# A block of two layers on one core: one weight ring of eight, a fourth pair by seven products, and low parts made by an adding DMA

## The chip, the cores and the metric

The kernel runs on one core of a Trainium2 chip. The core has five engines with queues of their own: TensorE (PE) multiplies matrices into PSUM, VectorE (DVE) and ScalarE (ACT) work elementwise, GpSimd (POOL) does some copies and issues DMAs, SyncE (SP) only issues DMAs. They meet at semaphores. 16 DMA engines move data. The metric is the device time of one execution in microseconds.

## What is computed

256 tokens of 2048 channels go through one transformer-like block and one mixer block, all in float32:

```python
h = rms_norm(x, norm_mix)
proj = h @ w_in                                   # 2048 x 11264
y_a = hgrn2_mixer(...); y_b = chunked_relpos_attention(...)
merged = gate_a * (y_a @ w_proj_a) + gate_b * (y_b @ w_proj_b)
x = x + merged @ w_out
h = rms_norm(x, norm_ffn)
ff_gate, ff_up = split(h @ w_ffn_in)              # 2048 x 11264
x = x + (silu(ff_gate) * ff_up) @ w_ffn_out       # 5632 x 2048
h = rmsnorm(x, a_norm_2)
u, v, gate = split(h @ a_w_in_2)                  # 2048 x 12288
v = rmsnorm(gelu(v), a_v_gain_2)
y = gelu(u) * (a_w_s_2 @ v + a_b_s_2)             # by groups of 512 channels
x = rmsnorm(x + (y * silu(gate)) @ a_w_out_2, final_norm_2)
```

## The kernel before

**Three matmuls for one.** Each float32 operand is written as a high part, rounded to the type fp32r, and a low part, the rest. A product is then high x high + low x high + high x low (`three` in the code): three matmuls. The activations' two parts stay in SBUF (`a_hi`, `a_lo`). The weights stream. A **unit** is a slab of 256 rows x 512 columns of weights (512 KB): a load into `raw`, then `split` on ScalarE copies it to `w_hi` (L615), `split` on VectorE subtracts to get `w_lo` (L1194), then TensorE uses it in 12 matmuls of 512 columns. `raw`, `w_hi` and `w_lo` are rings of `RING = 4` units. The high part of unit j+4 is made when unit j is used (`unit_used`), the load of unit j waits for the low part of unit j-4 (`lo_ready`, L485).

**Segments and steps.** All matrix work is a list of segments `S` (L347), each cut into steps of two column blocks. In form "D" the units of the two blocks alternate and two neighbouring units make a **pair**: feed-forward input (`FFN_IN`, 11 steps of 8 pairs), feed-forward output (`FFN_OUT`, 2 steps of 22), v (`V_IN`, 4 steps of 8), u and gate (`UG_IN`, 8 steps of 8), half of the last product (`Y_FIRST`), and a part of the input projection (`AV`).

**Seven products.** A pair is a 2x2 by 2x2 block product: 8 block products, 24 matmuls. Some pairs are done by seven (Strassen's scheme in Winograd's form), 21 matmuls, `mixed_pair`. The price lies on the other engines: four sums of weight blocks on VectorE (`weight_sums`, L1413 to L1416, from `raw` to `t_sum`, one of them in place in `raw`), their high part on ScalarE (`t_hi`, L746) and their low part on VectorE (`t_lo`, L1426), all in buffers for one pair. Sums of activation blocks (`s_sum`, `s_hi`, `s_lo`) are made once a stage. At the end of a step, `parts` (L1435 to L1438) and `whole` (L1450, two additions for each half) put the banks `mx` and `gp` together. Which pairs are done so is a table: `MIXED = (2, 4, 6)`, in step 0 of feed-forward input (4, 6), in step 0 of v (6,).

**The order** is written out by hand. Each engine has its own loop over units j = 0 to 15 of a step, calling `double_ahead` (work for unit j+4) and a `mid` function for what else falls there. The turn of the feed-forward output of step i-1 (eight transposes, `turn_ff`, L2226, into banks of `mx`, copied out by `ff_copy` on ScalarE) stands at unit 1 of step i. On GpSimd, the load of `ws_raw` (L589) waits until all activation parts of feed-forward input are made (`op_ready`), which the last `s_lo` (L1684) of row block 3 completes in step 0, and the load of `bs_all` comes next.

## Time and profile before

| | us |
|---|---|
| runs: median (lowest to highest of 3) | 2148.54 (2147.5 to 2149.36) |
| span of the profiled execution | 2146.8 |
| TensorE busy | 2135.6 (10176 matmuls) |
| VectorE busy | 1742.5 |
| ScalarE busy | 1261.2 |
| GpSimd busy | 138.1 |
| DMA | 412.35 MB, mean 192 GB/s |

The span goes from the first to the last instruction of one execution. Busy time counts an engine's own instructions; matmuls overlap in a pipeline, so a busy TensorE says little by itself, and the distance between the starts of two matmuls says what one costs. Shares over the whole span mix stages; the views of one step below say more.

### The profile page before, as it was taken

The page shows a single profiled execution, that of the slowest core. Times are in us where ns is not written, and L with a number is a line of the kernel's source. Part 1 is how long each engine was busy: PE and PEld are TensorE (multiplying, and loading weights), DVE is VectorE, ACT ScalarE, POOL GpSimd, SP SyncE. Part 2 cuts the span into 40 slices and gives each one's busy share as a digit, 9 for nine tenths or more (in the row PEclk, how much of TensorE's full clock was granted, in tenths as well). Part 3 has the DMA queues.
Part 4 walks back from the last instruction along what each step waited for, and adds up shares of the span by engine and source line. Part 5 has one row for each costly group of instructions (what it writes and reads, how often), then busy time and mean ns, then how long its engine had stood idle before and what let it go on. Part 6 is the DMA issues. An engine that isn't in the chain of part 4 may idle for free.

```text
span 2146.8 us, 30208 instructions
## 1 busy us (share of the span) xinstructions
PE 2135.6 (99%) x10176; PEld 1788.8 (83%) x10176; DVE 1742.5 (81%) x2125; ACT 1261.2 (59%) x1483; POOL 138.1 (6%) x218
## 2 busy tenths in 40 slices
PE   9999999999999999999999999999999999999998
PEld 9988888888888888888888888888888888888886
DVE  6578788666565698999899887787889999999886
ACT  6465455465544665555555555557667666666565
POOL 2022433101000000000000000000000000000000
PEclk9999999999999999999999999999999999999999
DMA  7666555575555566666666666666666666656664
GB/s 254 182 189 211 157 157 150 174 236 174 183 186 181 186 205 199 198 196 198 203 188 196 200 193 199 192 204 187 206 206 187 188 193 194 193 180 208 203 193 152
DMA packets 211513, 412.35 MB, mean 192 GB/s; under 512 B 13176, under 2 KB 13280, under 8 KB 211296
## 3 DMA queue, kind: packets, MB, share of 16 engines
q1 hardware_dynamic: 208608, 402.70, 60.9%
q0 software_dynamic: 1920, 5.31, 0.8%
q10 hardware_dynamic: 896, 3.15, 0.5%
q8 instruction: 55, 0.90, 0.2%
q14 instruction: 34, 0.28, 0.0%
HBM read 409.01 MB, written 3.16 MB: 192 GB/s over the span
## 4 chain that ended last, share of the span: by engine, by line
PE 96%; DVE 2%; DMA 1%; ACT 0%; issue 0%; DVEq 0%; SPq 0%; ACTq 0%
PE gp L1983 49%; PE gp L1915 33%; PE mx L1983 10%; PE mx L2226 1%; PE mx L2110 1%; DVE w_lo L1194 1%; DMA raw<-a_w_out_in 1%; PE mx L2275 1%; DVE t_lo L1426 0%; DVE ff_lo L1193 0%; PE mx L2113 0%; DMA x_tok<-x_in 0%; PE mx L2107 0%; PE mx L2162 0%; PE mx L2206 0%
## 5 line engine op out<-in xcount | busy, mean ns | idle before, releaser
L615 ACT ACTIVATE w_hi<-raw 128x1024 fp32r<-128x1024 f32 x759 | 797.1, 1056 | 681.6 <-PE gp L1915 246.3
L1194 DVE TENSOR_TENSOR w_lo<-raw,w_hi 128x1024 fp32r<-128x1024 f32 x759 | 921.2, 1230 | 233.8 <-ACT w_hi L615 224.1
L1983 PE MATMUL gp<-w_hi,a_hi 128*128 128x512 f32 x1053 | 413.3, 393 | 0.0
L1983 PE MATMUL gp<-w_lo,a_hi 128*128 128x512 f32 x1053 | 410.1, 389 | 0.0
L1983 PE MATMUL gp<-w_hi,a_lo 128*128 128x512 f32 x1053 | 409.8, 389 | 0.0
L1983 PEld LDWEIGHTS gp<-w_hi,a_hi 128*128 128x128 f32 x1053 | 197.7, 188 | 43.0 <-issue 2.9
L1983 PEld LDWEIGHTS gp<-w_lo,a_hi 128*128 128x128 f32 x1053 | 197.6, 188 | 41.4
L1983 PEld LDWEIGHTS gp<-w_hi,a_lo 128*128 128x128 f32 x1053 | 197.8, 188 | 39.8
L1915 PE MATMUL gp<-w_hi,a_hi 128*128 128x512 f32 x576 | 229.9, 399 | 0.0
L1915 PE MATMUL gp<-w_lo,a_hi 128*128 128x512 f32 x576 | 224.6, 390 | 0.0
L1915 PE MATMUL gp<-w_hi,a_lo 128*128 128x512 f32 x576 | 224.3, 389 | 0.0
L1983 PE MATMUL gp<-w_hi,ff_hi 128*128 128x512 f32 x410 | 159.9, 390 | 0.0
L1983 PE MATMUL gp<-w_lo,ff_hi 128*128 128x512 f32 x410 | 159.5, 389 | 0.0
L1983 PE MATMUL gp<-w_hi,ff_lo 128*128 128x512 f32 x410 | 159.5, 389 | 0.0
L1426 DVE TENSOR_TENSOR t_lo<-t_sum,t_hi 128x1536 fp32r<-128x1536 f32 x76 | 133.5, 1756 | 8.0 <-ACT t_hi L746 3.8
L1915 PEld LDWEIGHTS gp<-w_lo,a_hi 128*128 128x128 f32 x576 | 108.1, 188 | 23.1
L1915 PEld LDWEIGHTS gp<-w_hi,a_hi 128*128 128x128 f32 x576 | 108.2, 188 | 22.1 <-DVE w_lo L1194 0.4
L1915 PEld LDWEIGHTS gp<-w_hi,a_lo 128*128 128x128 f32 x576 | 108.3, 188 | 21.2
L746 ACT ACTIVATE t_hi<-t_sum 128x1536 fp32r<-128x1536 f32 x76 | 111.9, 1473 | 0.0
L1983 PEld LDWEIGHTS gp<-w_lo,ff_hi 128*128 128x128 f32 x410 | 76.9, 188 | 16.1
L1983 PEld LDWEIGHTS gp<-w_hi,ff_hi 128*128 128x128 f32 x410 | 77.0, 188 | 15.9
L1983 PEld LDWEIGHTS gp<-w_hi,ff_lo 128*128 128x128 f32 x410 | 77.0, 188 | 15.7
(420 smaller groups left out, 3305.3 us busy)
## 6 DMA issues: line engine op xcount, KB each, us to landing
raw<-a_w_in_in SPq DMA_DIRECT2D x192, 512.0 KB, 4.5
raw<-w_ffn_in_in SPq DMA_DIRECT2D x176, 512.0 KB, 4.5
raw<-w_in_in SPq DMA_DIRECT2D x175, 512.0 KB, 3.9
raw<-w_ffn_out_in SPq DMA_DIRECT2D x88, 512.0 KB, 4.6
raw<-a_w_out_in SPq DMA_DIRECT2D x64, 512.0 KB, 4.9
raw<-w_out_in SPq DMA_DIRECT2D x32, 512.0 KB, 4.0
raw<-w_proj_a_in SPq DMA_DIRECT2D x16, 512.0 KB, 4.6
raw<-w_proj_b_in SPq DMA_DIRECT2D x16, 512.0 KB, 4.7
```

The costliest lines, as they stand in the source:

```text
L615: act.activation(w_hi[:, slot], raw[:, slot], ACT.Copy).then_inc(hi_ready, 1)
L746: act.activation(t_of(k)[1][:], t_of(k)[0][:], ACT.Copy).then_inc(t_hi_ready, 1)
L1194: dve.tensor_tensor(w_lo[:, slot], raw[:, slot], w_hi[:, slot], ALU.subtract).then_inc(lo_ready, 1)
L1426: dve.tensor_tensor(t_of(k)[2][:], t_of(k)[0][:], t_of(k)[1][:].bitcast(F32), ALU.subtract).then_inc(t_lo_ready, 1)
L1915: ins = pe.matmul(out_, stat, mov, start=start, stop=last and p == 2, skip_group_check=True)
L1983: ins = pe.matmul(out_, stat[sp_], mov[mp], start=start and p == 0, stop=stop and p == 2, skip_group_check=True)
L2110: pe.matmul(part8[:, (l + 1) * P:(l + 2) * P], decay[buf][:, l, tb], decay[buf][:, l, tb], start=True, stop=True, skip_group_check=True)
L2226: ins = pe.transpose(turn_b[:, m, t * P:(t + 1) * P], src(t, m), ident[:])
L2275: ins = pe.matmul(mx[:, c // 2, t0:t0 + P], v_one[:, b, c * P:(c + 1) * P], ws_t[:, b, bass.ds(g, 1)].rearrange("p a n -> p (a n)"), start ...
```

## The change

1. **One ring of eight.** `raw` and `w_lo` become one ring of eight slots, `w_lo` written over `raw`; `w_hi` keeps four. A load of unit j waits until unit j-8 is used.
2. **The sums moved up.** `weight_sums` of a pair stands ahead of the low part before it, one `split` earlier.
3. **Pair 0 by seven products** (`MIXED_WIDE`) in every step but the first of feed-forward input and v. Its sums are made at the end of the step before. The additions `whole(1)` move from unit 15 to unit 13 of the order, ahead of `t_lo`. Row block 0 gets sums of activations too (`SUMS0`, `s0_hi`, `s0_lo`). The turn moves from unit 1 to unit 15 of step i.
4. **Four low parts a step by DMA** (`ADDED`: units 3, 7, 11, 15 of feed-forward input, from unit 7 of step 0 on). ScalarE writes minus the high part to `low` (two buffers), GpSimd issues a DMA that adds `raw` to it, TensorE does the unit's 8 matmuls with high weights first and its 4 with `low` last (`low_last`). On VectorE a `memset` of one column stands in its place, to keep the count of `lo_ready`.
5. The scratch for GpSimd's DMAs is set to 8192 bytes, the last step of v stands outside the loop on VectorE and ScalarE.

```diff
+MIXED_WIDE = (0, 2, 4, 6)
+ADDED = (3, 7, 11, 15)
+LOWS = 2
...
-        raw = new("raw", [RING, UK, NB])
+        raw_at = top[0]
+        raw = new("raw", [RAW, UK, NB])
+        w_lo = at("w_lo", [RAW, UK, NB], raw_at, F32R)
         w_hi = new("w_hi", [RING, UK, NB], F32R)
-        w_lo = new("w_lo", [RING, UK, NB], F32R)
...
-            return MIXED
+            return MIXED_WIDE if k in WIDE else MIXED
...
+        def coming(k, i, j):
+
+            u = (j + RING) // 2
+            if u in mixed(k, i):
+                return mixed(k, i).index(u)
+            if u == S[k].units and k in WIDE and not (isinstance(i, int) and i == S[k].steps - 1):
+                return len(mixed(k, i))
+            return None
...
+        def added(k, i, j):
+
+            first = isinstance(i, int) and i == 0
+            if k != FFN_IN or j < RING and first:
+                return None
+            if j >= S[k].pair:
+                if isinstance(i, int) and i == S[k].steps - 1:
+                    return None
+                j -= S[k].pair
+            return ADDED.index(j) if j in ADDED else None
...
-                    if (k, i) != (0, 0) or j >= RING:
-                        sp.wait_ge(lo_ready, after(k, i, j + 1 - RING))
+                    if (k, i) != (0, 0) or j >= RAW:
+                        sp.wait_ge(unit_used, after(k, i, j + 1 - RAW))
...
             pool.wait_ge(op_ready, op0[FFN_IN] + DT)
             pool.dma_start(ws_raw[:], a_w_s.rearrange("g p q -> p g q")).then_inc(ws_in, 16)
+            count = 0
+            for i in range(S[FFN_IN].steps):
+                for unit in ADDED:
+                    n = added(FFN_IN, i, unit)
+                    if n is not None:
+                        count += 1
+                        pool.wait_ge(neg_ready, count)
+                        pool.dma_start(low[:, n % LOWS].bitcast(F32), raw[:, raw_slot(FFN_IN, i, unit)], accum_op=ALU.add).then_inc(lo_added[n], 16)
...
             def ahead(k, i, j):
 
+                n = added(k, i, j + RING + 1)
+                if n is not None:
+                    act.wait_ge(raw_in[raw_slot(k, i, j + RING + 1)], raw_use(k, i, j + RING + 1))
+                    act.activation(low[:, n % LOWS], raw[:, raw_slot(k, i, j + RING + 1)], ACT.Copy, scale=-1.0).then_inc(neg_ready, 1)
...
-                if j == 1:
+                if j == S[FFN_IN].pair - 1:
                     ff_copy(i - 1)
...
-                if u in mixed(k, i) and half == 0:
-                    weight_sums(k, i, mixed(k, i).index(u), j)
-                split(j % RING, after(k, i, RING + j + 1), tiles_ahead(k, i, j))
+                n = coming(k, i, j)
+                if j == 0 and n is not None:
+                    weight_sums(k, i, n, j)
+                if j % 2 == 1 and coming(k, i, j + 1) is not None:
+                    weight_sums(k, i, coming(k, i, j + 1), j + 1)
...
+                if n is not None and j % 2 == 1:
+                    if early_whole(k, i) and j == S[k].pair - 3:
+                        whole(k, i, 1)
+                    dve.wait_ge(t_hi_ready, pairs(k, i, n + 1))
...
+            def low_last(k, i, u, half, n):
+
+                place, end = (2 * u + half) % RING, S[k].units - 1
+                for m in range(TB):
+                    for kk in range(UK):
+                        start = kk == 0 and starts(k, i, u, half, m)
+                        for q, stat in enumerate(operand(k, i, u, kk, m)):
+                            pe.matmul(gp[:, half, m], stat, w_hi[:, place, kk], start=start and q == 0, stop=False, skip_group_check=True)
+                pe.wait_ge(lo_added[n], added_times(i, n))
+                for m in range(TB):
+                    for kk in range(UK):
+                        ins = pe.matmul(gp[:, half, m], operand(k, i, u, kk, m)[0], low[:, n % LOWS, kk], start=False,
+                                        stop=u == end and kk == UK - 1, skip_group_check=True)
...
-                if j == 1:
-                    turn_ff(i - 1)
+                if j == S[FFN_IN].pair - 1:
+                    turn_ff(i - 1, i + 1)
```

**Three places in the instruction order.** VectorE, step 0 of feed-forward input, before; the `s_sum` rows are activation sums of row block 3, `s_lo` their low part, `t_sum` the weight sums of pair 4:

```order
L1677 TENSOR_TENSOR s_sum<-a_two,s_sum 128x128
L1194 TENSOR_TENSOR w_lo<-raw,w_hi 128x1024
L1684 TENSOR_TENSOR s_lo<-s_sum,s_hi 128x512
L1709 TENSOR_REDUCE small<-small 128x2
L1413 TENSOR_TENSOR t_sum<-raw 128x512
L1414 TENSOR_TENSOR raw<-raw 128x512
L1415 TENSOR_TENSOR t_sum<-raw,t_sum 128x512
L1416 TENSOR_TENSOR t_sum<-raw,t_sum 128x512
```

And now:

```order
L1766 TENSOR_TENSOR s_sum<-a_two,s_sum 128x128
L1488 TENSOR_TENSOR t_sum<-raw 128x512
L1489 TENSOR_TENSOR raw<-raw 128x512
L1490 TENSOR_TENSOR t_sum<-raw,t_sum 128x512
L1491 TENSOR_TENSOR t_sum<-raw,t_sum 128x512
L1262 MEMSET small 128x1
L1774 TENSOR_TENSOR s_lo<-s_sum,s_hi 128x512
L1799 TENSOR_REDUCE small<-small 128x2
```

The four weight sums moved ahead of `s_lo`, and the low part that stood there is a `memset`.

GpSimd, the same place, before, with the last copy of the attention ahead of it:

```order
L560 COPY v_head<-val 128x256
L580 REGISTER_ALU
L580 COMPARE_AND_BRANCH
L589 DMA ws_raw<-a_w_s_in 128x8x128
L591 DMA bs_all<-a_b_s_in 128x1024
```

And now:

```order
L621 COPY v_head<-val 128x256
L641 REGISTER_ALU
L641 COMPARE_AND_BRANCH
L650 DMA ws_raw<-a_w_s_in 128x8x128
L658 DMA low<-raw 128x1024 x43
L660 DMA bs_all<-a_b_s_in 128x1024
```

All 43 additions stand in the queue between the two loads.

VectorE, the end of a looped step of feed-forward input, before, from the last addition of `parts` on:

```order
L1438 TENSOR_TENSOR c_part<-c_part 128x512
L1444 ISA
L1450 TENSOR_TENSOR c_part<-gp,c_part 128x512 x2
L1188 REGISTER_ALU
L1194 TENSOR_TENSOR w_lo<-raw,w_hi 128x1024
L1188 REGISTER_ALU
L1194 TENSOR_TENSOR w_lo<-raw,w_hi 128x1024
L1444 REGISTER_ALU
L1450 TENSOR_TENSOR c_part<-gp,c_part 128x512 x2
L1188 REGISTER_ALU
L1194 TENSOR_TENSOR w_lo<-raw,w_hi 128x1024
```

And now:

```order
L1519 TENSOR_TENSOR c_part<-c_part 128x512
L1529 ISA
L1535 TENSOR_TENSOR c_part<-gp,c_part 128x512 x2
L1264 REGISTER_ALU
L1270 TENSOR_TENSOR w_lo<-raw,w_hi 128x1024
L1529 REGISTER_ALU
L1535 TENSOR_TENSOR c_part<-gp,c_part 128x512
L1531 REGISTER_ALU
L1535 TENSOR_TENSOR c_part<-gp,c_part 128x512
L1507 TENSOR_TENSOR t_lo<-t_sum,t_hi 128x1536
L1264 REGISTER_ALU
L1270 TENSOR_TENSOR w_lo<-raw,w_hi 128x1024
```

One low part fewer stands between the two pairs of final additions, and `t_lo` of the next step's pair 0 follows them.

## Rows read from the trace of the kernel before

**Rows 1.** The page's part 4: engines' shares of the chain that ended last.

```profile
PE 96%; DVE 2%; DMA 1%; ACT 0%; issue 0%; DVEq 0%; SPq 0%; ACTq 0%
```

**Rows 2.** TensorE's waits: line, who released it, us in total, times, longest.

```profile
PE mx L1947 <- DVE ones L1232: 1.3, 1, 1.3
```

**Rows 3.** TensorE in order of time: start, us, line, output<-inputs, count.

```profile
1108.14 0.39 PE L1983 MATMUL mx<-w_hi,a_hi 128*128 128x512 f32 x1
...
1112.90 0.39 PE L1983 MATMUL gp<-w_hi,a_hi 128*128 128x512 f32 x1
...
1123.88 1.03 PE L2226 MATMUL mx<-ident,wide 128*128 128x128 f32 x8
1124.67 0.48 PE L1983 MATMUL gp<-w_hi,a_hi 128*128 128x512 f32 x1
```

**Rows 4.** Two steps: us; busy of PE, PEld, DVE, ACT, POOL; clock; DMA; GB/s.

```profile
1081.06:1123.56 42.50, 42.50 (x193) 35.10 (x192) 38.58 (x42) 23.88 (x24) 0.00 (x0) 1.00 0.65 198
1532.52:1574.11 41.59, 41.59 (x184) 34.27 (x183) 36.96 (x41) 26.87 (x34) 0.00 (x0) 1.00 0.65 202
```

**Rows 5.** VectorE in order of time, around the end of a feed-forward step.

```profile
1106.21 1.76 DVE L1426 TENSOR_TENSOR t_lo<-t_sum,t_hi 128x1536 fp32r<-128x1536 f32 x1
...
1113.17 0.69 DVE L1435 TENSOR_TENSOR c_part<-mx,c_part 128x512 f32<-128x512 f32 x1 [1.15 <-PE gp L1983]
...
1116.14 1.29 DVE L1450 TENSOR_TENSOR c_part<-gp,c_part 128x512 f32<-128x512 f32 x2
1117.35 2.35 DVE L1194 TENSOR_TENSOR w_lo<-raw,w_hi 128x1024 fp32r<-128x1024 f32 x2
1119.62 1.28 DVE L1450 TENSOR_TENSOR c_part<-gp,c_part 128x512 f32<-128x512 f32 x2
...
1121.95 1.40 DVE L1740 SCALAR_TENSOR_TENSOR wide<-c_part,small,wide 128x512 f32<-128x512 f32 x2
1123.27 0.68 DVE L1413 TENSOR_TENSOR t_sum<-raw 128x512 f32<-128x512 f32 x1
...
1125.92 2.52 DVE L1194 TENSOR_TENSOR w_lo<-raw,w_hi 128x1024 fp32r<-128x1024 f32 x2
```

**Rows 6.** ScalarE in the same step: a high part, then t_hi.

```profile
1103.74 1.06 ACT L615 ACTIVATE w_hi<-raw 128x1024 fp32r<-128x1024 f32 x1 [3.18 <-DVE t_sum L1416]
1104.70 1.47 ACT L746 ACTIVATE t_hi<-t_sum 128x1536 fp32r<-128x1536 f32 x1
```

**Rows 7.** Step 0 of feed-forward input: ScalarE, VectorE twice, GpSimd, TensorE.

```profile
745.65 1.06 ACT L615 ACTIVATE w_hi<-raw 128x1024 fp32r<-128x1024 f32 x1 [0.17 <-ACT wide L956]
...
746.75 1.23 DVE L1194 TENSOR_TENSOR w_lo<-raw,w_hi 128x1024 fp32r<-128x1024 f32 x1 [3.42 <-ACT w_hi L615]
...
751.65 0.68 DVE L1684 TENSOR_TENSOR s_lo<-s_sum,s_hi 128x512 fp32r<-128x512 f32 x1
...
752.63 0.91 POOL L589 DMA_DIRECT2D ws_raw<-a_w_s_in  x1 [209.78 <-DVE s_lo L1684]
...
757.11 0.39 PE L1983 MATMUL gp<-w_lo,a_hi 128*128 128x512 f32 x1
```

**Rows 8.** DMA: loads' queue (packets, MB, share); issues with KB, us to landing.

```profile
q1 hardware_dynamic: 208608, 402.70, 60.9%
...
hankel<-ext POOLq DMA_DIRECT2D x1, 1024.0 KB, 11.8
...
hank<-hankel POOLq DMA_DIRECT2D x8, 128.0 KB, 2.2
...
ws_raw<-a_w_s_in POOLq DMA_DIRECT2D x1, 512.0 KB, 5.2
```

**Rows 9.** The end: busy us of each engine, granted clock, DMA share, GB/s.

```profile
2138.00:2140.00 2.00, 0.87 (x4) 0.38 (x2) 0.94 (x2) 0.31 (x1) 0.00 (x0) 1.00 1.02 408
2140.00:2143.00 3.00, 0.00 (x0) 0.00 (x0) 1.77 (x5) 1.65 (x4) 0.00 (x0) 0.92 0.06 23
2143.00:2146.80 3.80, 0.00 (x0) 0.00 (x0) 0.00 (x0) 0.00 (x0) 0.00 (x0) 0.50 0.69 269
```

More of the change, by code:

```diff
@@ L45 @@
 RING = 4
+RAW = 8
 LEVELS = 8
@@ L499, in _ @@
             for k in range(1, len(S)):
-                if S[k].steps == 1:
-                    load(k, 0)
+                if S[k].steps == 1 or S[k].pair % RAW:
+                    for i in range(S[k].steps):
+                        load(k, i)
                     continue
@@ L602, in _, with split @@
             own = Chain(act, act_self)
-            def split(slot, use, used, tiles=None):
+            def split(slot, use, used, place, tiles=None):
                 act.wait_ge(raw_in[slot], use)
@@ L766, in double_step @@
                     double_ahead(k, i, j)
-                    if j >= S[k].pair - 2 and half_done is not None:
+                    if j >= S[k].pair - 2 and half_done is not None and not (k == FFN_IN and j == S[k].pair - 1):
                         half = j - (S[k].pair - 2)
@@ L992, in mid @@
                         stat_hi(n, turn, gain)
-                    if j % units == 5 and n >= 1:
+                    if j % units == 5 and (n >= 1 or n == 0 and turn in SUMS0):
                         mixed_hi(n, turn)
@@ L1096, in _ @@
             double_step(V_IN, 0, v_out, v_first)
-            with act.Fori(1, S[V_IN].steps) as i:
+            with act.Fori(1, S[V_IN].steps - 1) as i:
                 own.enter(i - 1, 6)
                 double_step(V_IN, i, v_out, no_mid)
-                own.leave(S[V_IN].steps - 1)
+                own.leave(S[V_IN].steps - 2)
+            double_step(V_IN, S[V_IN].steps - 1, v_out, no_mid)
             act.sem_inc(sums, 1)
@@ L1438, in parts, with early_whole @@
                 dve.tensor_tensor(c_of(k)[:, 1], c_of(k)[:, 3], c_of(k)[:, 1], ALU.add).then_inc(parts_added, 1)
+            def early_whole(k, i):
+                return k in WIDE and coming(k, i, S[k].pair - 3) is not None
             def whole(k, i, half):
@@ L1488, in double_step @@
                             rows_with_parts(k, i)
+                    if early_whole(k, i) and j == S[k].pair - 1:
+                        double_ahead(k, i, j)
+                        mid(i, j)
+                        continue
                     sooner = k == FFN_IN and isinstance(i, int) and i == S[k].steps - 1
@@ L1701, in mid @@
                         stat_lo(n, turn, gain)
-                    if j % units == 6 and n >= 1:
+                    if j % units == 6 and (n >= 1 or n == 0 and turn in SUMS0):
                         mixed_lo(n, turn)
@@ L1998, in plain_pair @@
                 for half in range(2):
-                    slot = (2 * u + half) % RING
+                    slot, place = raw_slot(k, i, 2 * u + half), (2 * u + half) % RING
                     if u == 0:
                         pe.wait_ge(bank_free[half], freed(k, i))
+                    n = added(k, i, 2 * u + half)
+                    if n is not None:
+                        pe.wait_ge(hi_ready, after(k, i, 2 * u + half + 1))
+                        low_last(k, i, u, half, n).then_inc(unit_used, 1)
+                        mid(i, 2 * u + half)
+                        continue
                     pe.wait_ge(lo_ready, after(k, i, 2 * u + half + 1))
@@ L2004, in plain_pair @@
                         for kk in range(UK):
-                            ins = three(gp[:, half, m], operand(k, i, u, kk, m), [w_[:, slot, kk] for w_ in (w_hi, w_lo)],
-                                        u == 0 and kk == 0, u == end and kk == UK - 1)
+                            ins = three(gp[:, half, m], operand(k, i, u, kk, m), [w_hi[:, place, kk], w_lo[:, slot, kk]],
+                                        kk == 0 and starts(k, i, u, half, m), u == end and kk == UK - 1)
                         if u == end and m == 0:
```

152 lines of the change are left out of this document (95 added, 57 removed).

## The prediction

> **What bounds the kernel now.** I read the chain of waits first: 96% of the span is TensorE [rows 1]. Then TensorE's own waits: the longest in 2146.8 us is 1.3 us, and it is the start-up; the other four rows of that view add 2.0 us [rows 2]. So no wait can be removed: only fewer matmuls make this kernel shorter, and anything that makes TensorE wait even once is a loss that nothing returns. Third, the pitch of the matmuls: a pair by seven products runs from 1108.14 to 1112.90, 4.76 us for 21 matmuls, 0.227 us each [rows 3]. A plain pair of 24 is 5.44 us, a unit (half of it) 2.72 us. The turn of eight transposes costs 0.79 us (1123.88 to 1124.67) and makes the first matmul behind it 0.48 long for 0.39, 0.9 us in all [rows 3]. With them a step of feed-forward input is 183 x 0.227 + 0.9 = 42.4 us (42.5 in the windows), and a step of v is 41.6 us, with no turn [rows 4]. The same windows show who is next: VectorE, 38.6 of 42.5 and 37.0 of 41.6 us, while ScalarE has room.
>
> **What the change takes away.** Pair 0 goes to seven products in steps 1 to 10 of feed-forward input and in steps 1 to 3 of v: 13 pairs, 3 matmuls less in each, 39 x 0.227 = **8.84 us**. Each is on TensorE's path, so this is the whole gain. It is 0.41% of the time, and a measurement of this kernel can tell about 0.2% (4.3 us) from no change.
>
> **The ring of eight, the sums moved up, the sums for row block 0.** The load of unit j now waits until unit j-8 is used, where it waited for the low part of unit j-4, which itself follows that use by a copy on ScalarE and a subtraction on VectorE (1.06 and 1.14 us). So loads start some 2 us sooner. TensorE waited for no load, so this is worth 0; it covers the sums that now need their two raw units earlier. The four more small sums and a low part in two residual stages (some 1.8 us of VectorE each, by the rows of the same lines) fall where VectorE waits for ScalarE, at 0. Bounds: 0, since no later consumer waits there today, to 1 us.
>
> **VectorE in feed-forward input.** I priced one step from rows: a low part 1.14 (two in 2.27), a weight sum of four 2.65, t_lo 1.7, the parts 3.0, four final additions 2.4, the product 1.3 [rows 5]. Before: 16 low parts, 3 sums, 3 t_lo: 18.2 + 8.0 + 5.1 + 6.7 = 38.0, as the window has it. After, 12 low parts, 4 sums, 4 t_lo: 13.7 + 10.6 + 6.8 + 6.7 = 37.8 in a step of 41.7 (40.8 + 0.9). It fits in sum. Then the tight place, counted from the start of pair 6 (its row is at 1108.14). The parts start 5.0 later and end at 8.0, the first two final additions at 9.2 [rows 5]. Now come one low part (10.35), the other two final additions (11.55) and t_lo of the next pair 0 (13.3). TensorE ends unit 15 at 4.76 + 5.44 = 10.2, turns until 11.1 and asks for t_lo after 12 matmuls, at 13.8. Margin 0.5 us: 0 to pay, at worst 0.5 in each of ten steps.
>
> **VectorE in v.** No turn stands there, so TensorE asks at 12.9 for what is ready at 13.3 to 13.4. That is 0.5 us late at the entries of steps 1, 2 and 3. And the sum of a step is 18.2 + 10.6 + 6.8 + 3.0 + 2.4 = 41.0 us of VectorE against 40.8 of TensorE: no room left, since none of v's low parts goes to a DMA. I take 3 x 0.5 = **+1.5 us**, bounds 0 and 3.5 (then v gains nothing and loses a little). So v keeps 0.5 of its 2.0 us.
>
> **The four low parts by DMA, in steady steps.** ScalarE writes minus the high part, GpSimd issues a DMA that adds the raw weights, TensorE does the 8 high matmuls of that unit first and then waits. ScalarE has the time (1.06 us each, four a step, on 23.9). The shortest window is unit 7's. From the same origin: t_lo 13.3, low part 14.4, product 15.8, sums for pair 2 18.4; ScalarE then makes a high part (1.0), t_hi (1.4) and the negative (1.0): 21.8 [rows 5, 6]. TensorE reaches the low part of unit 7 at 11.1 + 4.76 + 5.44 + 4.76 + 2.72 + 8 x 0.227 = 30.6. So the DMA has **8.8 us**; units 3, 11 and 15 have 10 to 13. No adding DMA is in this trace. The nearest rows: 512 KB on GpSimd's queue, loads beside it, 5.2 us from issue to landing; 1 MB there, 11.8 us [rows 8]. An addition moves 512 KB but must read its target too. A load's own share of the DMA engines is 60.9% x 2146.8 us / 768 = 1.7 us [rows 8]; a second stream beside the loads adds 1.7 to 3.4, so I take 7 to 8.5 us: in time, 0 to pay. Bounds 5.2 (nothing) and 11.8 (3 us in each of ten steps).
>
> The Trainium skill speaks to both ends. Its "DMA: Bandwidth & Descriptors", Anatomy of one DMA, gives 2.0 us plus the bytes over 436 GB/s, 3.2 us for 512 KB by my estimate; the trace has 5.2, so I stay with the trace. Its "Collectives: The Full Stack", The bandwidth ceiling, says a DMA addition costs two source reads, not slow arithmetic, and halves the rate; no row here shows an addition.
>
> **The first of them, in step 0.** Here I part from the idea of the change. GpSimd's queue has the load of ws_raw ahead of all 43 additions, and that load waits for the last low part of row block 3 (s_lo). In the trace s_lo ran at 751.65 and the load was issued at 752.63, the next thing that GpSimd did [rows 7]. Now s_lo comes later: ScalarE makes the negative of unit 7 ahead of the high part that began at 745.65 (+0.9 for VectorE's row at 746.75), and the order puts the sums of pair 4 (2.65) ahead of s_lo, for the low part of 1.14 that stood there: +2.4 in all. s_lo ends near 754.9, ws_raw goes out at 755.0 and takes 0.9 of GpSimd [rows 7], the addition for unit 7 at 755.9. TensorE wants it at 757.1, the ninth matmul of unit 7 [rows 7]. ws_raw lands at 760.2, and the addition's 3.4 us of two streams behind it give 763.6: **+6.5 us**. Bounds: landing 5.2 after issue, 761.1, +4.0; 11.8 after issue, +10.6. Nothing hides it, since TensorE had no slack.
>
> **The clock.** Granted clock is 1.00 (2.4 GHz) all through, but when TensorE has ended (0.87 us busy in 2138 to 2140, nothing later) it is 0.92 in the mean of 2140 to 2143 and 0.50 (1.2 GHz) behind that [rows 9]. A stop of some 6 us may thus end at the lower level, where each 0.227 costs twice. No row shows a climb. Bounds 0 and a stretch of 6.5 us at half speed, 3.3; I take **+1.5**.
>
> **Sum.** -8.84 + 1.5 + 6.5 + 1.5 = +0.7 us on 2146.8. The median of the runs stands 1.7 us above that span: 2149.2, which I call 2149.
>
> **Rivals.** Faster: the addition of step 0 lands early, because the queue handles it beside ws_raw and a small DMA there (128 KB) landed in 2.2 us [rows 8]. With a stall of 0 to 2 us and no fall of the clock: -8.84 + 1.5 + 1 = -6.3, 2142. For it: the DMA engines moved 408 GB/s in the last outputs [rows 9], where the mean of a load here is 1.7 us for 512 KB; against it: 5.2 us for ws_raw in just this place.
>
> If the 3.2 us of the Trainium skill (DMA: Bandwidth & Descriptors, Anatomy of one DMA) held, the addition would land at 759.1, the stall would be 2.0 and the time 2143.2, on this rival's side.
>
> Slower, by late additions: from a landing over 8.8 us on, TensorE waits at unit 7 of each steady step. At 10 us it is 10 x 1.2 = 12, 2161; at 11.8 it is 30, 2179. For it: 1 MB took 11.8. Against it: the other three units have more room.
>
> Slower, by traffic: loads take 16 x 1.7 = 27.2 us of the DMA engines in 41.7; four additions of 3.4 make 40.8. If one costs over 3.6 the loads set the pace: at 4.5, 3.5 us x 10, 2184. Against it: packets are drawn out when queues share, and at 408 GB/s [rows 9] a load is 1.3 us.
>
> Slower, by VectorE: the margin of 0.5 in feed-forward input is used up by waits between instructions; 0.5 late in ten steps is +5, 2154.
>
> That the change does not do what it says is excluded: the order has the three matmuls less in the pair and the 43 DMAs.
>
> **Chances.** Forecast (2145 to 2153) 0.49; early landing 0.18; late additions 0.19; traffic 0.05; VectorE 0.08. The forecast's upper edge lies at the bound of "same". Faster by over 0.2% (below 2144.2): 0.19. Within: 0.49. Slower (above 2152.8): 0.32. Range 2142 to 2164: it leaves out half of the early case and the worse part of late additions and traffic, 0.2.
>
> **What would show it.** Forecast: one wait of TensorE of 4 to 10 us near 757, released by the DMA into low; waits of 0.3 to 0.6 us for t_lo at three entries of v; steps of 41.7 us in feed-forward input; 39 matmuls less. Late additions: ten waits at that DMA, one a step. Traffic: waits for raw and a DMA share near 1 there. The forecast is wrong if the first wait is missing or under 3 us, or if steady steps are over 42 us.

## The result, and the profile after

The changed kernel takes 2151.29 us (median of 20 runs) where the kernel before took 2147.49 in the same session: a ratio of 1.0016, 95% interval 1.001 to 1.0022, 3.8 us slower. This is less than the 0.2% at which the prediction drew its line for no change, and 2.3 us above the 2149.0 that it gave. One of the 20 runs was a slow one, at 2360.05 us and a lower clock; without it the median is 2151.28. The profiled execution has a span of 2149.2 us; before it was 2146.8. The spans differ by 2.4 us and the medians by 3.8, since the profiled execution before took 2148.54, 1.05 above its median, and that of the changed kernel 2150.84, 0.45 below. What follows accounts for the 2.4; the other 1.4 is scatter between executions, which these traces don't resolve.

TensorE has 10137 matmuls, 39 less. Its waits, in the view that answers to [rows 2] (line, who released it, us in total, times, longest):

```profile
PE gp L2101 <- DMA low<-raw: 7.6, 1, 7.6
PE mx L2074 <- DVE t_lo L1507: 1.6, 4, 0.7
PE mx L2038 <- DVE ones L1308: 1.3, 1, 1.3
...
PE mx L2350 <- DVE s_lo L1774: 0.5, 1, 0.5
...
PE gp L2074 <- DVE c_part L1535: 0.2, 1, 0.2
```

One wait of 7.6 us stands out. Three more rows are new: t_lo (four times), s_lo at a turn of feed-forward output, and c_part. The two waits of the last product for sf_lo that the kernel before had (their row stands with the experiment on the ring) are gone.

Step 0 of feed-forward input, where the long wait stands, in order of time: GpSimd's queue, then TensorE. It answers to [rows 7].

```profile
754.82 0.92 POOL L650 DMA_DIRECT2D ws_raw<-a_w_s_in  x1 [212.18 <-DVE s_lo L1774]
755.72 0.96 POOL L658 DMA_DIRECT2D low<-raw  x1
```

```profile
756.67 0.39 PE L2097 MATMUL gp<-w_hi,a_lo 128*128 128x512 f32 x1
764.64 2.08 PE L2101 MATMUL gp<-low,a_hi 128*128 128x512 f32 x4 [7.59 <-DMA low<-raw]
766.51 0.63 PE L2074 MATMUL mx<-w_hi,a_hi 128*128 128x512 f32 x1
766.94 0.63 PE L2074 MATMUL mx<-w_hi,a_lo 128*128 128x512 f32 x1
...
768.96 0.39 PE L2074 MATMUL mx<-w_hi,s_hi 128*128 128x512 f32 x1
769.19 0.39 PE L2074 MATMUL mx<-w_hi,s_lo 128*128 128x512 f32 x1
```

The load of ws_raw waits 212 us at the head of GpSimd's queue for s_lo; the addition follows 0.9 us later, although ScalarE made the negative at 745.37 to 746.43. Behind the wait nine matmuls start 0.43 to 0.47 us before the next one and a tenth 0.31; from 768.96 on the distance is 0.23 again. The windows of that stretch (us, then busy time of PE, PEld, DVE, ACT and POOL, granted clock, DMA share, GB/s) show why:

```profile
757.00:760.00 3.00, 0.05 (x1) 0.00 (x0) 2.82 (x6) 2.19 (x3) 0.87 (x1) 1.00 0.81 228
760.00:763.00 3.00, 0.00 (x0) 0.00 (x0) 2.93 (x5) 0.00 (x0) 0.00 (x0) 0.83 1.03 240
763.00:766.00 3.00, 1.36 (x3) 1.17 (x4) 0.22 (x2) 0.00 (x0) 0.00 (x0) 0.50 0.96 190
766.00:769.00 3.00, 3.00 (x9) 2.31 (x8) 0.00 (x0) 1.06 (x1) 0.00 (x0) 0.53 0.32 65
769.00:772.00 3.00, 3.00 (x15) 2.46 (x14) 1.50 (x2) 2.12 (x2) 0.00 (x0) 1.00 0.83 257
```

The clock goes to its lower level (0.50, 1.2 GHz) while TensorE stands, and is back by 769. A steady step (same columns) and v's entries (TensorE in order of time) answer to [rows 4]; last the issues of the DMAs (times, KB, us to landing):

```profile
829.48:871.19 41.71, 41.71 (x190) 34.63 (x189) 38.16 (x47) 29.23 (x30) 3.42 (x4) 1.00 0.89 252
```

```profile
1492.11 0.50 PE L2074 MATMUL gp<-w_hi,s_hi 128*128 128x512 f32 x1 [0.22 <-DVE c_part L1535]
...
1493.78 0.50 PE L2074 MATMUL mx<-t_hi,s_hi 128*128 128x512 f32 x1 [0.70 <-DVE t_lo L1507]
...
1535.13 0.50 PE L2074 MATMUL mx<-t_hi,s_hi 128*128 128x512 f32 x1 [0.26 <-DVE t_lo L1507]
```

```profile
raw<-w_ffn_in_in SPq DMA_DIRECT2D x176, 512.0 KB, 5.2
...
low<-raw POOLq DMA_DIRECT2D x43, 512.0 KB, 6.8
```

A steady step of feed-forward input takes 41.71 us, and TensorE does not wait in it. Each step of v after the first is entered with a wait.

For the experiments the program is cut at turns of TensorE (eight transposes) that stand in every kernel. "Feed-forward in" runs from the turn at 740.75 of the kernel before (740.52 after) to that at 1214.11 (1216.62); "v" from 1458.66 to 1660.46 (1461.95 to 1664.24). The time of a stretch is the difference of two starts in one trace, so what came earlier doesn't touch it. The medians come from five sessions, in which the kernel before had 2147.49 to 2148.19 us; the ratio is to the kernel before of the same session.

| kernel | feed-forward in | v | median us | ratio to before, 95% |
|---|---|---|---|---|
| before | 473.36 | 201.80 | 2147.49 | |
| after | 476.10 | 202.29 | 2151.29 | 1.0016 (1.001 to 1.0022) |
| no addition for unit 7 of step 0 | 466.28 | 202.34 | 2141.46 | 0.997 (0.9959 to 0.9982) |
| that addition ahead of ws_raw | 466.28 | 202.33 | 2141.44 | 0.997 (0.9958 to 0.9981) |
| TensorE kept busy in the wait | 474.09 | 202.32 | 2149.29 | 1.0009 (1.0 to 1.0018) |
| copies in place of additions | 475.23 | 202.32 | 2150.32 | 1.0012 (1.0002 to 1.0021) |
| v without pair 0 | 475.34 | 201.74 | 2150.36 | 1.0013 (1.0004 to 1.0022) |
| ring and moved sums only | 472.51 | 201.67 | 2146.72 | 0.9996 (0.9987 to 1.0005) |
| pair 0, no additions | 475.89 | 202.34 | 2150.93 | 1.0014 (1.0005 to 1.0023) |
| additions, no pair 0 | 472.55 | 202.11 | 2147.14 | 0.9996 (0.9987 to 1.0005) |
| three edits | 466.50 | 201.68 | 2140.01 | 0.9962 (0.995 to 0.9975) |
| three edits, again | 466.28 | 201.74 | 2139.98 | 0.9963 (0.9949 to 0.9976) |
| additions in v too | 466.28 | 202.18 | 2141.20 | 0.9969 (0.9957 to 0.9981) |
| v's chain cut short | 466.30 | 200.85 | 2139.84 | 0.9959 (0.9946 to 0.9973) |

### The profile page after: what moved, and what is told of

Read it like the earlier page. It is cut to its first block, busy times and chain, and to the rows that moved or that the text cites. A ratio compares the mean times of both kernels' runs of the same rounds, so it can differ in the third digit from the quotient of the medians.

```text
span 2149.2 us, 30041 instructions
## 1 busy us (share of the span) xinstructions
PE 2128.7 (99%) x10137; PEld 1783.0 (83%) x10137; DVE 1748.6 (81%) x2200; ACT 1325.7 (62%) x1545; POOL 174.5 (8%) x261
## 4 chain that ended last, share of the span: by engine, by line
PE 95%; DVE 3%; ACT 1%; DMA 1%; issue 1%; DVEq 0%; POOL 0%; SPq 0%; ACTq 0%
PE gp L2074 41%; PE gp L2006 33%; PE mx L2074 11%; PE gp L2097 3%; PE gp L2101 2%; PE mx L2350 1%; PE mx L2234 1%; PE mx L2399 1%; DVE w_lo L1270 1%; DMA low<-raw 0%; ACT w_hi L684 0%; DVE c_part L1535 0%; DVE t_lo L1507 0%; PE mx L2237 0%; DMA x_tok<-x_in 0%
## 5 line engine op out<-in xcount | busy, mean ns | idle before, releaser
L1270 DVE TENSOR_TENSOR w_lo<-raw,w_hi 128x1024 fp32r<-128x1024 f32 x716 | 867.3, 1230 | 243.3 <-ACT w_hi L684 231.2
L2074 PE MATMUL gp<-w_hi,a_hi 128*128 128x512 f32 x790 | 309.4, 392 | 0.0
L2074 PE MATMUL gp<-w_hi,a_lo 128*128 128x512 f32 x790 | 307.6, 389 | 0.0
L2074 PE MATMUL gp<-w_lo,a_hi 128*128 128x512 f32 x790 | 307.6, 389 | 0.0
L2006 PE MATMUL gp<-w_hi,a_hi 128*128 128x512 f32 x576 | 229.9, 399 | 0.0
L2006 PE MATMUL gp<-w_lo,a_hi 128*128 128x512 f32 x576 | 224.6, 390 | 0.0
L2006 PE MATMUL gp<-w_hi,a_lo 128*128 128x512 f32 x576 | 224.3, 389 | 0.0
L2074 PEld LDWEIGHTS gp<-w_lo,a_hi 128*128 128x128 f32 x790 | 148.4, 188 | 31.1
L2074 PEld LDWEIGHTS gp<-w_hi,a_hi 128*128 128x128 f32 x790 | 148.5, 188 | 30.7 <-DVE w_lo L1270 0.2
L2074 PEld LDWEIGHTS gp<-w_hi,a_lo 128*128 128x128 f32 x790 | 148.5, 188 | 30.3
L1507 DVE TENSOR_TENSOR t_lo<-t_sum,t_hi 128x1536 fp32r<-128x1536 f32 x89 | 156.1, 1754 | 8.3 <-ACT t_hi L817 5.0
L817 ACT ACTIVATE t_hi<-t_sum 128x1536 fp32r<-128x1536 f32 x89 | 131.5, 1477 | 2.6 <-PE gp L2074 2.5
L2006 PEld LDWEIGHTS gp<-w_lo,a_hi 128*128 128x128 f32 x576 | 108.1, 188 | 23.3
L2006 PEld LDWEIGHTS gp<-w_hi,a_hi 128*128 128x128 f32 x576 | 108.2, 188 | 22.0 <-DVE w_lo L1270 0.4
L2006 PEld LDWEIGHTS gp<-w_hi,a_lo 128*128 128x128 f32 x576 | 108.3, 188 | 21.2
```

The lines of the kernel that those rows point to most:

```text
L817: act.activation(t_of(k)[1][:], t_of(k)[0][:], ACT.Copy).then_inc(t_hi_ready, 1)
L1270: dve.tensor_tensor(w_lo[:, slot], raw[:, slot], w_hi[:, place], ALU.subtract).then_inc(lo_ready, 1)
L1507: dve.tensor_tensor(t_of(k)[2][:], t_of(k)[0][:], t_of(k)[1][:].bitcast(F32), ALU.subtract).then_inc(t_lo_ready, 1)
L2006: ins = pe.matmul(out_, stat, mov, start=start, stop=last and p == 2, skip_group_check=True)
L2074: ins = pe.matmul(out_, stat[sp_], mov[mp], start=start and p == 0, stop=stop and p == 2, skip_group_check=True)
```

## The experiments

**The addition of step 0: cause and price.** Two kernels take the long wait away, in two ways. The first leaves out the one addition:

```diff
-            if k != FFN_IN or j < RING and first:
+            if k != FFN_IN or j < 2 * RING and first:
...
-            return i * 16 + 16 * (ADDED[n] >= RING)
+            return i * 16 + 16 * (ADDED[n] >= 2 * RING)
```

> Unit 7 of feed-forward input's step 0 has its low part made by VectorE again, and no DMA adds there; the 42 other additions stay. The theory: the whole loss is the wait of 7.6 us at unit 7 and the ten matmuls behind it at the half clock (0.43 to 0.47 us apart where 0.227 is the rule, 2.05 us in all). So the span falls by 9.7, from 2149.2 to about 2139.5, the median to about 2141.6, 0.27% under the kernel before, and the granted clock reads 1.00 from 757 to 772. A wait of up to 1 us on VectorE's low part may stand there instead, as its last sums of step 0 end at 754.5. The rival, that the additions of the other steps slow the transfers or VectorE, leaves more than half of the loss: 2145 or more.

Measured: span 2139.8, median 2141.46. The wait and the fall of the clock are gone; no wait for a low part stands there instead. The rival falls: feed-forward in is 9.82 us shorter, which is the whole loss, and the kernel is 6.1 us under the kernel before (2147.57 in its session).

The second keeps the addition and only issues it first:

```diff
-            pool.wait_ge(op_ready, op0[FFN_IN] + DT)
-            pool.dma_start(ws_raw[:], a_w_s.rearrange("g p q -> p g q")).then_inc(ws_in, 16)
             count = 0
...
                         pool.dma_start(low[:, n % LOWS].bitcast(F32), raw[:, raw_slot(FFN_IN, i, unit)], accum_op=ALU.add).then_inc(lo_added[n], 16)
+                        if count == 1:
+                            pool.wait_ge(op_ready, op0[FFN_IN] + DT)
+                            pool.dma_start(ws_raw[:], a_w_s.rearrange("g p q -> p g q")).then_inc(ws_in, 16)
```

> GpSimd issues the addition for unit 7 of step 0 ahead of the load of ws_raw, whose wait for the last row sums (they end at 754.5) it no longer stands behind. If the place in GpSimd's queue is the cause, the addition is issued when ScalarE's negative is made, at about 746.5, lands 6.0 to 8.9 us later, by 755.4 at the latest, and TensorE wants it at 757.1: wait and clock fall go, the median is about 2141.6 as with no addition there. If the addition is slow by itself there (beside the loads of that stretch), it lands after 757.1 and a wait stays: with 10 us of landing none, with 15 us 4 us of wait and most of the clock's 2 us, 2147.

GpSimd's queue and the clock of that kernel:

```profile
746.93 0.92 POOL L656 DMA_DIRECT2D low<-raw  x1 [204.12 <-ACT low L692]
755.01 0.95 POOL L659 DMA_DIRECT2D ws_raw<-a_w_s_in  x1 [7.17 <-DVE s_lo L1775]
```

```profile
760.00:763.00 3.00, 3.00 (x15) 2.48 (x14) 2.93 (x5) 1.67 (x2) 0.00 (x0) 1.00 1.08 297
763.00:766.00 3.00, 3.00 (x15) 2.49 (x14) 2.86 (x5) 2.55 (x3) 0.00 (x0) 1.00 1.02 298
```

The addition is issued 8.8 us sooner, at 746.93, and lands 7.5 us later by the view of DMAs, at 754.4; ws_raw goes out where it did. Nothing waits: 2141.44, 9.85 us under the changed kernel and the same as with no addition there. So the cause is shown: the place behind a load that itself waits. The rival, an addition that is too slow by itself there, falls with it. Within the wait of the changed kernel 1.4 us are a slower landing (8.9 us for 7.5) beside the load of ws_raw; they cost nothing once the addition is issued in time.

**The clock.** Dummy matmuls ahead of the wait:

```diff
+                if isinstance(i, int) and i == 0 and n == 1:
+                    for q in range(32):
+                        pe.matmul(mx[:, 0], a_hi[:, 0, 0:P], w_hi[:, place, 0], start=True, stop=True, skip_group_check=True)
                 pe.wait_ge(lo_added[n], added_times(i, n))
```

> 32 matmuls whose results nobody reads (128x512, 0.227 us each, 7.3 us in all) stand on TensorE ahead of the wait for unit 7's addition in step 0. The addition lands no sooner, so the stop is as long, but TensorE works through it. If the clock falls because TensorE stands still, it reads 1.00 from 757 to 772, the matmuls behind go at 0.227, and the time falls by 2.05 us: span 2147.1, median about 2149.2. The rival, that the clock falls there for another reason (the load that starts at 754.8, the stage itself), leaves the time at 2151 and the clock at 0.50 in that stretch.

TensorE in order of time:

```profile
758.93 7.42 PE L2100 MATMUL mx<-w_hi,a_hi 128*128 128x512 f32 x32
766.57 1.21 PE L2104 MATMUL gp<-low,a_hi 128*128 128x512 f32 x4 [0.22 <-DMA low<-raw]
767.62 0.40 PE L2074 MATMUL mx<-w_hi,a_hi 128*128 128x512 f32 x1
767.85 0.39 PE L2074 MATMUL mx<-w_hi,a_lo 128*128 128x512 f32 x1
```

The stop is as long, filled with work for nothing; the clock reads 1.00 in each window from 757 to 772 and the matmuls behind go at 0.23. The stretch is 2.01 us shorter and the median 2.00. The span of the profiled execution (2149.2) doesn't show it, since this execution came to the stretch 2.0 us later (742.55 for 740.52). The clock falls because TensorE stands still, and it cost 2.0 us; the wait cost the rest, 7.7 by the starts of the matmuls on either side of it (756.67 and 764.64, less one pitch).

**What the addition costs the DMA engines.** The additions become copies, so this kernel leaves the additions out:

```diff
-                        pool.dma_start(low[:, n % LOWS].bitcast(F32), raw[:, raw_slot(FFN_IN, i, unit)], accum_op=ALU.add).then_inc(lo_added[n], 16)
+                        pool.dma_start(low[:, n % LOWS].bitcast(F32), raw[:, raw_slot(FFN_IN, i, unit)]).then_inc(lo_added[n], 16)
```

> The 43 additions by DMA are plain copies of the same 512 KB (so the low parts of these units are wrong: this kernel leaves the additions out). The theory, that the second read costs: each lands in about 5.2 us (as ws_raw did, 512 KB too) where it was 6.8, the queue's share of the engines' time falls from 6.8% to about half, and the wait at unit 7 from 7.6 to about 6.0: span 2147.6, median 2149.7. The rival, that start and row count set the landing and not the addition, leaves it at 6.5 to 7 and the time at 2151.

The page's queue and issues of that kernel:

```profile
q0 software_dynamic: 8112, 27.86, 3.6%
```

```profile
low<-raw POOLq DMA_DIRECT2D x43, 512.0 KB, 5.3
```

With additions the same line reads 6.8%, with as many packets and bytes. The kernel before had 0.8% on this queue, ws_raw and hankel of [rows 8] among it, so 43 copies take 2.8% and 43 additions 6.0% of 16 engines' span: 1.4 and 3.0 us of all engines for one. Landing falls from 6.8 to 5.3 us in the median, the long wait from 7.6 to 6.4: near what was expected (5.2 and 6.0). Feed-forward in is 0.87 us shorter, and the median 2150.32 where 2149.7 was expected. The 1.2 us that the wait lost are what an addition costs there over a copy; with a plain copy in the same place in the queue 6.4 remain. The run takes away the second read and the arithmetic together, so it doesn't show which of the two costs.

The Trainium skill says in "Collectives: The Full Stack", The bandwidth ceiling, that a collective that adds is slower than one that copies for its two source reads and not for the arithmetic, with a measured ratio of 1.93 between them. The ratio of engine time here, for DMAs of one core, is 6.0 to 2.8, 2.1: the size agrees, the reason no run here shows. The 3.2 us for a 512 KB copy that the prediction estimated from the Trainium skill ("DMA: Bandwidth & Descriptors", Anatomy of one DMA) stand beside 5.3 measured with loads running; here the measurement decides.

**Pair 0 and the additions, each alone.** The ring and the sums moved up stay in all three kernels. The first has neither pair 0 nor additions (MIXED everywhere, no units by DMA, no sums over row block 0):

```diff
-ADDED = (3, 7, 11, 15)
+ADDED = ()
...
-        SUMS0 = (TURN_H2, TURN_H3, )
+        SUMS0 = ()
...
-        WIDE = (FFN_IN, V_IN,)
+        WIDE = ()
```

> Of the change only the ring of eight and the sums and last additions moved up: no pair 0, no additions by DMA, no sums over row block 0. The theory, that moving the weight sums one place up is what took away the two waits of the last product for its sums (0.56 and 0.32 us in the kernel before, each with a slower matmul behind it): the time is 1.4 us below the kernel before, ratio 0.9993. The rival, that these waits went by the later start of that stretch: ratio 1.0000.

Its span is 2144.7, 2.1 below the kernel before, and its median 1.2 below. The interval of the ratio (0.9987 to 1.0005) holds both what was expected and the rival, so the time decides nothing; the trace shows where the span went. TensorE's waits of the kernel before, behind 1975 us:

```profile
PE mx L1983 <- DVE sf_lo L1429: 0.9, 2, 0.6
```

This kernel has no wait there, and it comes to that stretch 1.2 us sooner than the kernel before, so the rival (a later start) falls. VectorE at the first of the two places, in the kernel before and then in this one:

```profile
2001.09 0.29 DVE L1408 TENSOR_TENSOR sf_sum<-y_all 128x128 f32<-128x128 f32 x1 [1.29 <-DMA raw<-a_w_out_in]
```

```profile
1996.87 0.28 DVE L1483 TENSOR_TENSOR sf_sum<-y_all 128x128 f32<-128x128 f32 x1
```

Before, VectorE stood still 1.29 us there (1.04 at the second place) until the load of the pair's weights had landed; now it doesn't. So two parts of the change can have taken TensorE's waits away, the ring, by which loads start sooner, and the sums moved up. They were not separated. Feed-forward in is 0.85 shorter, a step 42.39 for 42.48 us.

Then pair 0 without additions:

```diff
-ADDED = (3, 7, 11, 15)
+ADDED = ()
```

> No additions by DMA: VectorE makes all low parts, pair 0 stays in both products. In a step of feed-forward input VectorE's busy time rises from 38.1 us by four low parts of 1.22 us less four markers, to 42.8, over TensorE's 41.7: with its idle a step of 43.0, 1.3 us more in each of ten steps, 13 us, against the 9.7 us of wait and clock in step 0 that go: span 2152.5, median about 2154.6. The rival, that VectorE has slack enough and the additions bring nothing: 2141.6 as without unit 7's addition.

A step takes 42.56 us in the mean of nine (turn to turn). VectorE is busy 41.89 us in a window of 42.60:

```profile
1081.00:1123.60 42.60, 42.55 (x189) 34.30 (x188) 41.89 (x47) 25.12 (x26) 0.00 (x0) 1.00 0.65 197
```

The step is as long as before the change (42.48), though it has three matmuls less; VectorE is busy 98% of it and sets it. Feed-forward in takes 9.6 us more than with the additions well placed. I had put the step at 43.0, half a microsecond too much, since I added idle time to a VectorE that has almost none.

Then the additions (first one ahead of ws_raw) without pair 0, the other two lines of the diff above:

> The ring, the sums moved up and the additions by DMA (the first ahead of the load of ws_raw), but no pair 0 anywhere. TensorE sets the step, so VectorE's relief brings nothing by itself: the time is that of the ring alone, 2146.7, a step of feed-forward input 42.4. The rival, that the additions' traffic costs by itself, gives 0.1 us or more a step: 2147.8 or more; if VectorE's relief were worth something without pair 0, 2145 or less.

Feed-forward in takes 472.55 us, where the ring alone took 472.51. So in that stretch the additions cost nothing and bring nothing by themselves; they are what lets pair 0 count. (v takes 202.11 us in this kernel and 201.67 with the ring alone: TensorE waits 0.4 us for a low part at 1633.32. Why only here is open.) With both, 466.28: 6.3 us for 30 matmuls that are worth 6.8.

**v.** Its pair 0 alone is taken back:

```diff
-        WIDE = (FFN_IN, V_IN,)
+        WIDE = (FFN_IN,)
```

> v goes without pair 0 and all else stays. By v's own steps (four starts of pairs that wait for t_lo or c_part, 2.8 us in all, against 9 matmuls of 0.227 us) the time falls by 0.5 us, to 2150.8: no difference to be measured. The rival, that the matmuls saved in v count in full and the stops would stand elsewhere anyway, makes it slower by 2.0 us: 2153.3.

v takes 201.74 us without pair 0 and 202.29 with it, although it has nine matmuls more: 0.55 us less, as expected. The stretch repeats well enough to say so: 202.29 to 202.34 in the six kernels of the table that have pair 0 in v and nothing else changed there. (The medians differ by 0.9, but they can't be read for v: feed-forward in, which this edit leaves alone, is 0.76 shorter in this trace, with a long wait of 7.3 for 7.6.) So this part of the change costs more than it brings.

Why v is late at its entries was the open question, with two answers: VectorE is full (40.8 us busy of 41.5), or the wait ends a fixed chain. Four low parts a step by the adding DMA in v as well, with the first of all additions ahead of ws_raw:

```diff
-            if k != FFN_IN or j < RING and first:
+            if k not in (FFN_IN, V_IN) or j < RING and first:
...
+            for i in range(S[V_IN].steps):
+                for unit in ADDED:
+                    n = added(V_IN, i, unit)
+                    if n is not None:
+                        count += 1
+                        pool.wait_ge(neg_ready, count)
+                        pool.dma_start(low[:, n % LOWS].bitcast(F32), raw[:, raw_slot(V_IN, i, unit)], accum_op=ALU.add).then_inc(lo_added[n], 16)
```

> The addition for unit 7 of step 0 goes ahead of the load of ws_raw; both products keep pair 0; and v too has four low parts a step made by the adding DMA (its low parts leave VectorE, 1.22 us each). The theory, that v's pair 0 brings nothing because VectorE is then busy 40.8 of v's 41.4 us: its two waits of 0.26 us for t_lo and the one of 0.70 at its entry go, the one for c_part stays, and of the nine matmuls' 2.04 us about 2.0 is seen. From turn to turn v takes 200.3 us, where it was 202.3 with and 201.7 without pair 0; the median is 2139.4, 2 us under the kernel with the additions reordered alone. The rival, that additions in v collide with its loads, or wait in GpSimd's queue behind the load of bs_all: v stays at 202 or more, 2141.5 or more.

My theory fell. VectorE is busy 36.8 us of a step now, and TensorE waits as before:

```profile
1525.64 0.50 PE L2083 MATMUL mx<-t_hi,s_hi 128*128 128x512 f32 x1 [0.26 <-DVE t_lo L1516]
```

VectorE at this entry, in order of time:

```profile
1517.33 0.69 DVE L1525 TENSOR_TENSOR c_part<-mx,c_part 128x512 f32<-128x512 f32 x1 [1.15 <-PE gp L2083]
...
1520.30 1.29 DVE L1544 TENSOR_TENSOR c_part<-gp,c_part 128x512 f32<-128x512 f32 x2
1521.51 1.21 DVE L1279 TENSOR_TENSOR w_lo<-raw,w_hi 128x1024 fp32r<-128x1024 f32 x1
1522.64 1.28 DVE L1544 TENSOR_TENSOR c_part<-gp,c_part 128x512 f32<-128x512 f32 x2
1523.84 1.75 DVE L1516 TENSOR_TENSOR t_lo<-t_sum,t_hi 128x1536 fp32r<-128x1536 f32 x1
```

VectorE stands idle 1.15 us before the chain and runs without a gap in it. TensorE's last product of pair 6 starts at 1516.84 and is through at 1517.07; the chain begins 0.26 later and ends, with t_lo, at 1525.59: 8.5 us in all. (In the changed kernel, with VectorE busy right up to it, the chain began the same 0.26 behind the products.) TensorE has 5.44 us of plain units and 12 x 0.227 = 2.7 of pair 0 to do meanwhile, 8.2, and in feed-forward input the turn on top. That turn is why t_lo is in time there and late here. The changed kernel has a check of this in itself: the entry of step 1 of feed-forward input, at 791.25, is the one that has no turn ahead of it, and the one there at which TensorE waits for t_lo.

The chain cut short, with v's additions taken out again (the last of v's four final additions is left out but for one column):

```diff
-                    ins = dve.tensor_tensor(c_of(k)[:, c], gp[:, half, m], c_of(k)[:, c], ALU.add)
+                    cols = slice(0, 1) if k == V_IN and (half, m) == (1, 1) else slice(0, NB)
+                    ins = dve.tensor_tensor(c_of(k)[:, c, cols], gp[:, half, m, cols], c_of(k)[:, c, cols], ALU.add)
```

> The additions reordered (unit 7 of step 0 first), pair 0 in both products, no additions by DMA in v; in v the last of the four final additions (c_part, 0.64 us) adds one column of 512 only, so a quarter of v's sums is wrong: this leaves work out to shorten one chain. The theory, formed after additions in v left the waits as they were to 0.01 us: t_lo of v's pair 0 is late by the chain that hangs on the end of pair 6 (four sums of the parts, four final additions, one low part, t_lo), whatever VectorE has to do before it. Shortened by 0.6, the two waits of 0.26 at the entries of steps 2 and 3 go with the slow starts beside them (0.53 each), that for c_part too (0.49), and that of 0.70 falls to 0.1 to 0.2 (0.6): v takes 200.2 us from turn to turn for 202.3, the median is 2139.3. The rival, that something outside this chain (ScalarE's t_hi, the loads) releases TensorE there: the waits stay and the time is 2141.4.

```profile
PE mx L2076 <- DVE t_lo L1508: 1.0, 2, 0.7
PE mx L2352 <- DVE s_lo L1776: 0.5, 1, 0.5
```

Of the four waits for t_lo the two of 0.26 are gone (the one of 0.3 in this row is feed-forward input's), and that for c_part as well. v takes 200.85, 1.45 us less. That of 0.68 at the entry of step 1 stays, which I had at 0.1 to 0.2. I had counted one gain twice. The two last additions take 0.53 us less (0.75 for 1.28), so t_lo ends 0.53 sooner; but the wait for c_part, which stood ahead of it, is gone too, so TensorE asks for t_lo 0.5 sooner and waits as long. The entry in all is 0.53 shorter (its shifts add up to 1.26 for 1.79): what the chain lost, once. Beside this, the chain starts 1.3 us later there (1.55 behind the products, at 1475.72, for 0.26): ScalarE, which must first copy two of the parts, has waited 2.51 us for a small operation of VectorE, and VectorE comes without a gap from the sums and low parts of v's start. Which of the two holds it was not separated. The theory holds at all three entries; at the first one the chain also begins late, for another reason.

**A version that beats both kernels.** The addition issued first, v without pair 0, and no sums over row block 0 at the turns of feed-forward output, which only v's pair 0 read:

```diff
-        SUMS0 = (TURN_H2, TURN_H3, )
+        SUMS0 = (TURN_H2,)
```

> Three edits together: the addition for unit 7 of step 0 is issued ahead of the load of ws_raw; v goes without pair 0 (feed-forward input keeps it); and the sums over row block 0 at the turn in feed-forward output are left out, since only v's pair 0 read them. By the trace of the changed kernel: 9.7 us for the first, 0.5 for the second (v's stops cost 2.8 us where nine matmuls save 2.04, and 0.3 of slow starts come back), 0.6 for the third (the wait of 0.49 us at 1344.24 and the slow matmul behind it). Span 2149.2 - 10.8 = 2138.4, median about 2140.5, 0.33% under the kernel before. If the parts overlap with other waits, 2142.

2140.01 us, 0.38% under the kernel before. Behind 700 us this kernel has one wait left:

```profile
PE mx L2075 <- DVE t_lo L1508: 0.3, 1, 0.3
```

Once more, beside the kernel with additions in v:

> The kernel with the three edits (the addition of unit 7 first, v without pair 0, no sums over row block 0 in feed-forward output) once more, beside the one with additions in v, on the same chip: 2140.0 as before. By the theory of VectorE's load the kernel with additions in v is 0.6 us faster than this one, by the rival 1.5 us slower.

2139.98 against 2141.20: with VectorE relieved v's pair 0 still costs 1.2 us, 0.5 in v (202.18 for 201.7) and the rest at the turn of feed-forward output.

## Why the prediction was right

Its sum was made of a gain that is certain and a stall that eats it; both are there. That it came so near is luck in part: smaller terms were wrong in both directions, as the sum at the end of this section shows. Step by step:

**Matmuls, -8.84: right.** 39 less. In feed-forward input a step is 42.48 - 41.71 = 0.77 us shorter, 0.68 of it from three matmuls and 0.1 from the ring.

**The first addition, +6.5 (4.0 to 10.6): right in mechanism, 1.1 too small.** ws_raw was issued at 754.82 (I had 755.0) and the addition at 755.72 (755.9). It landed 8.9 us after its issue, at about 764.6, where I had 763.6; that was the slowest of the 43, whose median is 6.8. I counted 3.4 us from the landing of ws_raw, at 760.2. But ws_raw itself took 6.5 us here, not the 5.2 of [rows 8]: it landed at 761.3, and 3.4 behind that is 764.7. Why it was slower is not shown. The addition beside it can't be all of it, since ws_raw took 6.0 us in the two kernels without additions.

**The clock, +1.5 (0 to 3.3): right, 2.0 measured.** The prediction had no row for how it comes back; it was back 4.3 us after the work went on.

**Steady additions, 0: right.** 6.0, 6.8 and 8.9 us to landing (least, median, most) in a window of 8.8, and the slowest was that of step 0. Late additions and traffic, which held 0.24 of the chances, did not come. The DMA share is 0.89 in a step, and TensorE waits for no load.

**VectorE in feed-forward input, 0: right** but for one entry, that of step 1, of 0.33 us (0.6 with its slow start). The prediction counted a turn ahead of each of the ten entries; the first has none.

**v, +1.5 for stops: too small, by 1.** The step that failed priced three waits of 0.5 and nothing else. Starts of matmuls in order of time show that an entry costs more than its wait: at 1535.13 the wait is 0.26, the start comes 0.42 later than the pitch asks and the next one 0.11, 0.53 in all. At the entry of step 1 two waits stand (c_part 0.22, t_lo 0.70) and the shifts add up to 1.8. So v's stops are 2.8, 0.3 of such small shifts that the kernel before had go, and v loses 0.5 us where I let it keep 0.5. The reason given, that no turn covers the chain, was right. The other one, that VectorE has no room left in v, was not: the experiment with additions in v took it away and nothing changed.

**Sums for row block 0, 0: wrong, 0.65, inside its bound of 1.** The row is TensorE's, at a turn of feed-forward output:

```profile
1344.24 1.09 PE L2350 MATMUL mx<-ident,wide 128*128 128x128 f32 x8 [0.49 <-DVE s_lo L1774]
```

The stretch from the turn before to this one takes 12.45 us, where it took 11.80. The transposes wait for `op_ready`. For row block 0 VectorE's a_lo gave that count before; in the changed kernel the later s_lo gives it. I looked at what VectorE had to do and not at who waits for the count that now comes later; the 0 rested on "no later consumer waits there today". Without these sums the wait is gone.

**Ring and moved sums, 0: wrong, to the good side.** The last product's two waits for sf_lo, 0.56 and 0.32 us, were in the view that I read as one where "no wait can be removed". They went with the ring and the moved sums. The prediction gave the ring nothing because TensorE waited for no load, but VectorE did, 1.29 and 1.04 us ahead of the sums that TensorE then waited for. With the matmuls that start slowly behind the waits it is 1.4 us from the last turn to the last matmul: 161.82 us for 163.22, both in the changed kernel and in the one with the ring alone. (That one's span shows only 0.9 of it, because its last outputs landed 0.5 us later: 8.89 us from the last matmul to the end, 8.37 in the changed kernel.)

In the span: -8.84 + 7.7 + 2.0 (first addition and clock) + 2.5 (v) + 0.65 (sums) + 0.6 (first entry of feed-forward input, with its slow start) - 0.85 and - 1.4 (ring) = +2.4, and 2149.2 - 2146.8 is 2.4. So the forecast of +0.7 was near by luck, because errors of either sign stood in it: 1.7 too little for the first addition and the clock, 1.0 for v, 1.25 for the sums and the first entry, against 2.25 of gain that I did not see: 1.7 in sum, from +0.7 to +2.4.

## What to carry to other kernels

A DMA put on a queue inherits every wait of what stands ahead of it: list for each queue what it waits for and when, before adding to it. Here one place in a queue was worth 9.8 us, more than the whole gain of the change, and moving it costs nothing. Relief for a busy engine helps only where its busy time sets the pace: where a short chain hangs on the last result of another engine, count that chain link by link against what the other has to do meanwhile. Where one engine holds 96% of the chain that ended last, the other 4% are still worth a look by name, and so is what the engine that it waits for was waiting for: 0.9 us of TensorE's waits stood behind VectorE's waits for loads, and went with an edit made for something else. Two waits in series are one gain: shorten the chain behind both, and only its end counts.

## What the runs showed of the hardware

- An adding DMA within SBUF (512 KB) took 6.0 to 8.9 us to land with loads beside it, 6.8 in the median, and by my estimate from the queue's share 3.0 us of all 16 engines' time; a plain copy of the same data took 5.3 in the median and by the same estimate 1.4. Loads of feed-forward weights landed in 5.2 us beside additions and in 3.7 to 3.8 in the two kernels with the larger ring and no additions.
- GpSimd needed 0.86 us to issue an addition and 0.53 for the copy.
- TensorE's granted clock was 1.00, then 0.83, then 0.50 in three windows of 3 us from 757 on, in which it stood still from 756.9 to 764.6; it was 1.00 again behind 769, after 4.3 us of work. Nine matmuls went at 0.43 to 0.47 us and one at 0.31. With idle work in the gap it stayed at 1.00.
- A matmul released late, by t_lo or c_part, started some 0.16 us later than its wait shows, and the next one 0.11 late (four places of v: 0.16 or 0.17, and 0.11).
